# Paired experts: up slots fetched two at a time, and two groups of products exchanged on TensorE

## What is computed

```python
def moe_swiglu(x, w_router, w1, w3, w2):
    t = x.reshape(bn * s, d)
    logits = (t @ w_router).astype(jnp.float32)
    top_val, top_idx = lax.top_k(logits, TOP_K)              # TOP_K = 2 of N_EXPERTS = 8
    top_w = jax.nn.softmax(top_val, axis=-1)
    combine = jnp.sum(jax.nn.one_hot(top_idx, N_EXPERTS) * top_w[..., None], axis=1)
    for e in range(N_EXPERTS):
        out = out + combine[:, e:e + 1] * ((jax.nn.silu(t @ w1[e]) * (t @ w3[e])) @ w2[e])
```

## Time and profile before

| | us |
|---|---|
| median of three executions | 2334.82 (2331.53 to 2339.3) |
| span of the profiled execution, first to last instruction | 2336.6 |
| of it TensorE busy | 2273.0 (97%) |
| of it VectorE busy | 1490.8 (64%) |
| of it ScalarE busy | 959.5 (41%) |
| bytes read from device memory | 653.76 MB, 280 GB/s over the span |

### The profile page before, as it was taken

One profiled execution on the slowest core, in us unless ns is written; L12 is line 12 of the kernel. 1 busy time (PEld: TensorE's weight loads), 2 busy tenths in 40 slices (PEclk: granted clock), 3 DMA queues, 4 the chain that ended last, 5 costly groups with the idle time before them and its releaser, 6 DMA issues.

```text
span 2336.6 us, 37077 instructions
## 1 busy us (share of the span) xinstructions
PE 2273.0 (97%) x14964; PEld 1904.1 (81%) x14964; DVE 1490.8 (64%) x1853; ACT 959.5 (41%) x1149; POOL 45.9 (2%) x37
## 2 busy tenths in 40 slices
PE   6999999998999999999999998999999999999999
PEld 4889998877667677666766666888999999988998
DVE  6945885974555555555555554564799788864664
ACT  3215343213444544444444442323433566654342
POOL 0100000100000000000000000020000000000000
PEclk9999999999999999999999999999999999999999
DMA  9755894865999999999999994412688344433552
GB/s 403 305 201 199 348 370 180 328 240 211 386 421 412 421 419 415 392 421 416 404 410 420 413 421 173 144 37 100 265 359 342 131 155 141 141 124 116 189 182 90
DMA packets 90431, 656.85 MB, mean 281 GB/s; under 512 B 10032, under 2 KB 10288, under 8 KB 10800
## 3 DMA queue, kind: packets, MB, share of 16 engines
q1 hardware_dynamic: 82800, 603.26, 65.2%
q10 hardware_dynamic: 7488, 51.59, 5.4%
HBM read 653.76 MB, written 1.05 MB: 280 GB/s over the span
## 4 chain that ended last, share of the span: by engine, by line
PE 86%; DVE 5%; DMA 4%; issue 2%; ACT 2%; SPq 0%; DVEq 0%; ACTq 0%
PE bank L1447 85%; DMA ring<-stream_dram 2%; DMA work<-stream_dram 2%; DVE ring_rounded L2364 1%; DVE work L2376 1%; PE bank L2029 1%; DVE rstd L2445 0%; DVE ring L2376 0%; PE bank L1853 0%; DVE xT L2370 0%; PE bank L2068 0%; DVE work L2367 0%; ACT work_rounded L1097 0%; DVE ff_mid L2370 0%; DVE yT L2370 0%
## 5 line engine op out<-in xcount | busy, mean ns | idle before, releaser
L2364 DVE TENSOR_TENSOR ring_rounded<-ring,work_rounded 128x2048 fp32r<-128x2048 f32 x223 | 518.1, 2325 | 295.0 <-ACT work_rounded L1097 176.4
L1447 PE MATMUL bank<-work_rounded,proj_rounded 128*128 128x512 f32 x1000 | 310.7, 409 | 2.3 <-DVE ring_rounded L2364 2.3
L1447 PE MATMUL bank<-h_heads_rounded,work_rounded 128*128 128x256 f32 x1344 | 279.6, 281 | 0.0
L1447 PE MATMUL bank<-yT_rounded,ring_rounded 128*128 128x256 f32 x960 | 271.4, 283 | 0.0
L1447 PE MATMUL bank<-hT,ring 128*128 128x256 f32 x1088 | 248.3, 388 | 15.6 <-ACT hT L973 9.2
L1447 PEld LDWEIGHTS bank<-hT,ring 128*128 128x128 f32 x1088 | 209.5, 194 | 54.7 <-issue 10.2
L1447 PEld LDWEIGHTS bank<-work_rounded,proj_rounded 128*128 128x128 f32 x1000 | 191.0, 192 | 48.2 <-issue 2.7
L1447 PEld LDWEIGHTS bank<-h_heads_rounded,work_rounded 128*128 128x128 f32 x1344 | 221.0, 189 | 3.0 <-issue 2.9
L1447 PEld LDWEIGHTS bank<-yT_rounded,ring_rounded 128*128 128x128 f32 x960 | 184.0, 192 | 0.0
L1090 ACT ACTIVATE work_rounded<-ring 128x2048 fp32r<-128x2048 f32 x86 | 164.4, 1912 | 11.5 <-DMA ring<-stream_dram 11.4
L1447 PE MATMUL bank<-work_rounded,ff_hid_rounded 128*128 128x512 f32 x508 | 160.4, 408 | 2.2 <-DVE work_rounded L2364 2.2
(11 more groups left out here) (337 smaller groups left out, 4220.4 us busy)
## 6 DMA issues: line engine op xcount, KB each, us to landing
ring<-stream_dram SPq DMA_DIRECT2D x477, 1024.0 KB, 7.7
work<-stream_dram SPq DMA_DIRECT2D x92, 1024.0 KB, 9.3
work<-stream_dram ACTq DMA_DIRECT2D x48, 1024.0 KB, 8.9
params<-params_dram SPq DMA_DIRECT2D x1, 1728.5 KB, 25.9
consts<-consts_dram SPq DMA_DIRECT2D x1, 1568.0 KB, 31.4
xT<-x_dram SPq DMA_DIRECT2D x1, 1024.0 KB, 5.7
out_dram<-xT SPq DMA_DIRECT2D x1, 1024.0 KB, 3.9
consts<-consts_dram SPq DMA_DIRECT2D x1, 577.0 KB, 29.8
```

Of the source, the lines that this page charges most:

```text
L1447: return pe.matmul(o, lhsT=a, rhs=b, start=start, stop=stop, skip_group_check=True)
L2364: return dve.tensor_tensor(o, a, b, op)
```

## The change

1. **Up slots in pairs.** The two up slots of an expert's chunk are laid out in device memory so that each of the 128 partitions has its 16 KB in one row, and they are fetched by one DMA of 2 MB (`expert_up`) instead of two of 1 MB. The DMA waits until both places are free. Two neighbouring places of the ring are one contiguous piece of SBUF (`two_slots`); for this the places are shifted by one (`pair_place`).
2. **Semaphores by kind.** Arrivals are counted per kind of slot (many, few, few down, many down) and parity of the step. A half of an up pair no longer has an arrival of its own: `up_high_of` and `few_up_products` wait for the pair.
3. **Order.** On TensorE `few_up_products(s)` comes ahead of `few_down(s - 1)`. `pair_slot` and the order of the loads follow: many pair, few pair, few down, many down.
4. `load_again` reads halves of the 16 KB rows; it is skipped here.

```diff
@@ pair_slot
-        return 6 * s + (6 if what == "few_down" else 9)
+        return 6 * s + (8 if what == "few_down" else 9)
...
-    return 6 * s + {"many": -2, "few": 1}[what]
+    return 6 * s + {"many": -2, "few": 0}[what]
@@ semaphores and places
-        def pair_here(s, what, half=0):
-            n = pair_slot(s, what) + half
-            return pair_arrived[n % PAIR_RING], 16 * (n // PAIR_RING + 1)
+        def pair_here(s, what):
+            return pair_arrived[what][s % 2], 16 * (s // 2 + 1)
...
+        def pair_place(i):
+            return (moe_first - 1 + i) % RING
+
+        def two_slots(i):
+            if i >= RING:
+                return work[:, moe_n + 6 * SLOT:moe_n + 8 * SLOT]
+            return ring[:, pair_place(i):pair_place(i) + 2, :].rearrange("p a n -> p (a n)")
@@ load_experts
-                def expert_slot(s, what, half=0):
...
-                    n = pair_slot(s, what) + half
-                    if n >= PAIR_RING:
-                        sp.wait_ge(weights_used, moe_first + n - PAIR_RING + 1)
-                    part = 3 * c + (2 if what.endswith("down") else half)
-                    sp.dma_start(pair_ring(s, what, half),
-                                 stream_in[bass.ds(first_of[e] + part, 1)].rearrange("a p n -> p (a n)"))\
-                      .then_inc(pair_arrived[n % PAIR_RING], 16)
+                def expert_up(s, what):
...
+                    n = pair_slot(s, what)
+                    if n >= PAIR_RING:
+                        sp.wait_ge(weights_used, moe_first + n - PAIR_RING + 2)
+                    sp.dma_start(two_slots(n % PAIR_RING),
+                                 stream_in[bass.ds(first + 3 * c, 2)].rearrange("a p n -> (a p n)")
+                                 .rearrange("(p n) -> p n", p=P)).then_inc(pair_arrived[what][s % 2], 16)
...
                 for s in range(PAIR_STEPS):
-                    for half in range(2):
-                        expert_slot(s, "many" if s else "few", half)
+                    expert_up(s, "many" if s else "few")
+                    expert_up(s, "few" if s else "many")
                     if s:
-                        expert_slot(s - 1, "few_down")
-                    for half in range(2):
-                        expert_slot(s, "few" if s else "many", half)
-                    if s:
-                        expert_slot(s - 1, "many_down")
+                        expert_down(s - 1, "few_down")
+                        expert_down(s - 1, "many_down")
@@ ACT, up_high_of
-                    act.wait_ge(*pair_here(s, "many", half))
+                    act.wait_ge(*pair_here(s, "many"))
@@ TensorE, few_up_products
+                    pe.wait_ge(*pair_here(s, "few"))
                     for half in range(2):
-                        pe.wait_ge(*pair_here(s, "few", half))
@@ TensorE, order of a step
                     many_up(s)
+                    few_up_products(s)
                     few_down(s - 1)
-                    few_up_products(s)
                     many_turn(s)
@@ lay_stream
-                    stream[at + 3 * c:at + 3 * c + 2] = both.reshape(P, 2, SLOT).transpose(1, 0, 2)
+                    stream[at + 3 * c:at + 3 * c + 2] = both.reshape(2, P, SLOT)
```

More of the change, by code:

```diff
@@ L485, in build_program @@
                         " twice few room excess most flag pick den inv w pc0 pc1 cb0 cb1")
-        pair_arrived = [sem(f"pair_arrived{i}") for i in range(PAIR_RING)]
+        pair_arrived = {what: [sem(f"{what}_arrived{i}") for i in range(2)]
+                        for what in ("many", "few", "few_down", "many_down")}
         again_here = [sem(f"again_here{i}") for i in range(RING)]
@@ L678, in pair_ring @@
                 return (more_slots_r if rounded else more_slots)[i - RING]
-            return (ring_r if rounded else ring)[:, (moe_first + i) % RING, :]
+            return (ring_r if rounded else ring)[:, pair_place(i), :]
+        def pair_place(i):
[4 more added lines that the diff above has]
+            return ring[:, pair_place(i):pair_place(i) + 2, :].rearrange("p a n -> p (a n)")
         def rounds_at(at):
@@ L770, in load_experts @@
                                           max_val=moe_first + EXPERT_SLOTS * (EXPERTS - 1)) for i in range(EXPERTS)]
-                def expert_slot(s, what, half=0):
+                def expert_up(s, what):
                     pair, c = divmod(s, EXPERT_CHUNKS)
-                    e = pair if what.startswith("many") else PAIRS + pair
-                    n = pair_slot(s, what) + half
+                    first = first_of[pair if what == "many" else PAIRS + pair]
+                    n = pair_slot(s, what)
[4 more added lines that the diff above has]
+                                 .rearrange("(p n) -> p n", p=P)).then_inc(pair_arrived[what][s % 2], 16)
@@ L776, in expert_slot, with expert_down @@
+                def expert_down(s, what):
+                    pair, c = divmod(s, EXPERT_CHUNKS)
+                    first = first_of[pair if what == "many_down" else PAIRS + pair]
+                    n = pair_slot(s, what)
                     if n >= PAIR_RING:
                         sp.wait_ge(weights_used, moe_first + n - PAIR_RING + 1)
-                    part = 3 * c + (2 if what.endswith("down") else half)
-                    sp.dma_start(pair_ring(s, what, half),
-                                 stream_in[bass.ds(first_of[e] + part, 1)].rearrange("a p n -> p (a n)"))\
-                      .then_inc(pair_arrived[n % PAIR_RING], 16)
+                    sp.dma_start(pair_ring(s, what),
+                                 stream_in[bass.ds(first + 3 * c + 2, 1)].rearrange("a p n -> p (a n)"))\
+                      .then_inc(pair_arrived[what][s % 2], 16)
@@ L792, in load_experts @@
-                expert_slot(PAIR_STEPS - 1, "few_down")
-                expert_slot(PAIR_STEPS - 1, "many_down")
+                        expert_down(s - 1, "few_down")
+                        expert_down(s - 1, "many_down")
+                expert_down(PAIR_STEPS - 1, "few_down")
+                expert_down(PAIR_STEPS - 1, "many_down")
             def load_again():
@@ L803, in expert_slot @@
                         sp.wait_ge(again["used"], e * EXPERT_SLOTS + (n - RING + 1))
-                    sp.dma_start(ring[:, (moe_first + at) % RING, :],
-                                 stream_in[bass.ds(e * EXPERT_SLOTS + (moe_first + part), 1)].rearrange("a p n -> p (a n)"))\
+                    from_slot = e * EXPERT_SLOTS + moe_first + part
+                    if part % 3 == 2:
+                        rows = stream_in[bass.ds(from_slot, 1)].rearrange("a p n -> p (a n)")
+                    else:
+                        half = part % 3
+                        rows = stream_in[bass.ds(from_slot - half, 2)].rearrange("a p n -> (a p n)")\
+                            .rearrange("(p n) -> p n", p=P)[:, half * SLOT:half * SLOT + SLOT]
+                    sp.dma_start(ring[:, (moe_first + at) % RING, :], rows)\
                       .then_inc(again_here[(moe_first + at) % RING], 16)
```

## The result

The changed kernel takes 2377.2 us (median of four, 2374.14 to 2379.81) against 2334.74 of the kernel before in the same comparison: a ratio of 1.0182, 95% interval 1.0164 to 1.020. It is slower by 42 us; 15 were predicted, 26 at most. The profiled span is 2374.4 us, 37.8 more than before. Lines move by 22: the helpers' L1447 and L2364 are now L1469 and L2386, the turns L2051 and L2090, `up_high_of` and `down_high_of` L1112 and L1119; pairs are loaded in L788, down slots in L798.

A forecast was written before the change was run, and what follows sets the result against it. TensorE was taken as the bound, on a load lead eaten in plain steps and refilled in side steps. Terms 12.6 - 0.9 (old stalls gone) + 2.5 + 0.7 = +14.9 us gave 2350; own range 2342 to 2357, with rivals 2337 to 2361.

The forecast's parts named there:

- What bounds the kernel: Paired experts stage: TensorE bounds it; loads fall 0.68 us behind per plain step and gain 1.05 in scatter steps.
- Arithmetic: TensorE, ACT and DVE work in the stage: same products, exchanging few up and few down costs 0, bounds -0.1 and +0.1 a step.
- Rate of a pair: Up loads in 16 KB rows: 425 GB/s, 4.94 us a pair, so 14.86 us of loads a step.
- What a pair costs in lead: Ring of up slots: later asking and later news cut the lead of the loads from 5.1 us to 0.4 us.
- Its own sign of being wrong: Changed kernel's trace: plain steps still 14.30 with long up-slot waits, or pair landings under 4.6 or over 5.0 us apart.
- How many steps pay: Runs of plain steps and four transposition steps: those paying are lengthened by 12.6 us in sum, 8.9 to 16.1.
- The clock: TensorE at the stage's start: a longer idle gap may lengthen the lower-clock part, 0 to 1.7 us, taken as 0.7.
- The start: First many up of the stage: ACT waits for the whole pair, +2.5 us, plus 0.7 for the clock.
- The third: Up loads: 16 KB rows move as two of 8 KB, 2353, or slower, some 2365; beyond 2357 had 0.08.
- The second: Up loads: wide rows much faster, loads never lag, only the start is left, 2336; 0.19 together with the first rival.

The follow-up runs named there:

- few_single: Changed kernel, but the few up slots come as two 1 MB DMAs, each asked for and told of by itself; many pair unchanged: 2356.2 us, ratio 1.0097.
- order_only: Changed kernel's new order, but each up slot has its own 1 MB DMA in 8 KB rows, asked for and told of singly: 2335.0 us, ratio 0.9996.
- late_ask: Changed kernel's order with 1 MB up loads in 8 KB rows, told one by one, asked for only when both places are free: 2346.0 us, ratio 1.0055.
- ring_ten: Changed kernel with ten ring places instead of eight, made by keeping one copy of the many up slots' high parts: 2338.7 us, ratio 1.0009.

## Why the prediction was wrong, by its own steps

- **What bounds the kernel: right.** Loads fall behind in plain steps, and side steps refill. few_single, where a pair is told of late and the queue stays filled, pays in plain steps of 14.85 us, against 14.86 forecast.
- **Arithmetic: right** (order_only, 0).
- **Rate of a pair: right.** It was taken as 4.94 us; queued pairs land 4.90 apart. The median packet of 16 KB takes 611 ns, one of 8 KB 309.
- **What a pair costs in lead: the step that failed.** The prediction let the few pair land "at 6.2 + 4.8 + 2.5 = 13.5", 7.3 us after the ask, which gave 0.4 us of lead, and said that once it is eaten "each plain step lasts as long as its loads". The runs show 9.2 instead of 7.3 (median of 53 few pairs, 7.5 to 11.0). The 4.8 was read as the landing of a load that found an empty queue (one row). But the load ahead of that one, issued at 946.35 in the trace of before, landed 8.0 later, at 954.3, 1.5 us after the ask at 952.86:

```profile
ring<-stream_dram SPq DMA_DIRECT2D x1, 1024.0 KB, 8.0
```

  In the changed kernel the pair ahead lands 3.6 us after the ask (median); the few pair then needs its own 4.9, and some 0.7 more because it was asked for so shortly ahead. The prediction's own figures told against 13.5: once the many pair lands 9.1 into a step, as its line ends, a pair behind it in the queue that takes 4.94 lands at 14.0. With 9.2 the loop lasts 30.2 us instead of some 28.2, more than two steps of loads (29.7) or of products (28.6). So plain steps are not as long as their loads, 14.86, but as long as half the loop: the 21 that pay without a drop of the clock last 15.3 us on average. Its own sign of being wrong was there too: few pairs land more than 5.0 us behind the load ahead (5.9 in the loop above).
- **How many steps pay: right, at the wrong price.** Some 24 plain steps and four with the transposition were expected; 23 of the 30 steps in the table's count pay, 28.1 us in all instead of 12.6. Of that some 11 us is what the forecast had (loads at 14.86 us a step, in 21 steps), 9.5 is the loop beyond that (15.3 instead of 14.86), and 7.4 lies in two steps with a drop of the clock. The other steps, held to be unchanged, pay another 8.6, 10 of them by over 0.2 us.
- **The clock: missed.** Two of the waits are followed by a drop to the lower level, 1.2 GHz. The first, timeline and window:

```profile
916.42 0.30 PE L2090 MATMUL bank<-consts,hT 128*128 128x128 f32 x1 [1.92 <-DVE ff_hid_rounded L2386]
```

```profile
916.42:920.00 3.58, 3.58 (x12) 3.00 (x13) 2.05 (x1) 0.87 (x2) 0.00 (x0) 0.53 1.05 446
```

  With the wait itself this is the step of 18.39 us, 3.7 over its 14.70; the other is at 1363.52, also after 1.92 of idling, also +3.7. Together 7.4 of the 36.7 us, the waits included.
- **The start: right in sum.** 2.5 for the landing and 0.7 for the clock were forecast; many up starts at 572.21, 3.14 later than before, and the clock over it is 0.81 against 0.80, so the second term is nothing and the first larger. Turn 0 is 2.99 late:

```profile
572.21 0.77 PE L1469 MATMUL bank<-work_rounded,proj_rounded 128*128 128x512 f32 x1 [5.16 <-DVE ring_rounded L2386]
```

- **The rivals.** The third came nearest in time (2365, rows slower than two slots) for a reason that the runs exclude. The second, much faster rows, needed a pair in 4.65 us or less; two queued slots take 2 x 2.48 = 4.96 us and a queued pair 4.90, so joining them saves 0.06. None had two delays that are harmless or small alone and close a loop together. The range ended at 2361 because its upper end was made of rates and counts, with no bound on the time from ask to landing other than one row.

## What to carry to other kernels

A transfer that is asked for later, and a landing that is told of later, are not only lead spent: follow the chain from the ask through the landing, the engines and the freed place back to the next ask, add it up, and compare it with what the steps in it take by rate. When the chain is the longer, it sets the pace, and the sign of it is steps that last longer than their loads need (here 15.1 to 15.3 us against 14.86). A DMA share that falls over the whole stage is a weaker sign, since it also falls in steps whose products take longer than their loads. Give the ask more room (here two places more) before blaming size or layout.

## What the runs showed of the hardware

How far ahead a load has to be asked for. Spacing of landings beyond the 4.90 us of a queued pair or the 2.48 of a queued slot, mean, by how long before the landing of the load ahead it was issued (600 to 1400 us, from issue and landing of each load):

| issued ahead of that landing by | changed kernel (pairs and slots) | late_ask (1 MB) |
|---|---|---|
| under 2.6 us | 2.28 (13 loads) | 1.90 (5) |
| 2.6 to 4.4 | 0.56 (27) | 0.64 (18) |
| 4.4 to 5 | 0.17 (14) | 0.05 (14) |
| over 5 | 0.07 (146) | 0.02 (274) |

So a load asked for 3.7 us before the one ahead has landed still lands half a microsecond or more late, whether it is 1 MB or 2. With shorter notice the engines are seen partly idle while the earlier load is still landing: from the ask of a few pair at 1338.42 to 1340.57, where the load ahead landed, their share is 0.74:

```profile
1338.42:1340.57 2.15, 2.15 (x22) 1.44 (x20) 1.87 (x2) 0.25 (x1) 0.00 (x0) 1.00 0.74 213
```

With 3.7 us of notice, in the loop shown above, it was 0.98, so most of the loss there is not idling; the mean packet of 16 KB takes 649 ns in the changed kernel's stage and 629 in ring_ten's. What the engines wait for (their own unequal ends, or the start of the next load) was not tried. Nor is it settled why a wait of 1.92 us was followed by the lower clock at 916 and 1364 and one of 1.95 at 821.12 was not.
